# Another start for the top-k search, and one pass for its last places

## The reference

```python
s = jnp.einsum('bthd,bsd->bths', qi, ki)
score = jnp.einsum('bth,bths->bts', wi, jax.nn.relu(s))
visible = jnp.arange(L)[None, :] < limit[:, None]       # limit: the end of the row's chunk of 64
score = jnp.where(visible[None], score, -jnp.inf)
top_val, top_idx = lax.top_k(score, top_k)              # 256 of up to 2048; 144 of 576 for the sample
...
logits = jnp.einsum('btjgd,btnjd->btjgn', qg, k_sel) * (HEAD_DIM ** -0.5)
p = jax.nn.softmax(logits, axis=-1)
```

## Time and profile before

| | |
|---|---|
| median of three runs | 3711.19 us |
| span of the profiled execution | 3702.1 us |
| TensorE busy | 3263.2 us, 88% |
| VectorE busy | 2260.1 us, 61% |
| ScalarE busy | 1078.5 us, 29% |
| GpSimd busy | 785.9 us, 21% |
| mean granted TensorE clock | 0.952 |

### The profile page before, as it was taken

One profiled execution on the slowest core, in us unless ns is written; L12 is line 12 of the kernel. 1 busy time (PEld: TensorE's weight loads), 2 busy tenths in 40 slices (PEclk: granted clock), 3 DMA queues, 4 the chain that ended last, 5 costly groups with the idle time before them and its releaser, 6 DMA issues. The chain is left out here.

```text
span 3702.1 us, 51508 instructions
## 1 busy us (share of the span) xinstructions
PE 3263.2 (88%) x19482; PEld 2934.2 (79%) x19482; DVE 2260.1 (61%) x4788; ACT 1078.5 (29%) x1854; POOL 785.9 (21%) x404
## 2 busy tenths in 40 slices
PE   3999985787888887888789999999979899999997
PEld 2777764566666665667689999999969899999997
DVE  5667672777777766684226656656531666666654
ACT  2222222455455544444212221221221211211221
POOL 0000002111000000000245433433214434434420
PEclk7999996999999998999889999999989899999999
DMA  4122225221111010000321111111132211111101
GB/s 138 63 93 84 76 86 151 55 55 33 49 28 28 28 28 25 14 15 13 114 86 35 57 45 34 57 45 34 33 113 75 69 35 45 57 34 45 57 11 48
DMA packets 164909, 202.67 MB, mean 55 GB/s; under 512 B 27775, under 2 KB 138660, under 8 KB 162596
## 3 DMA queue, kind: packets, MB, share of 16 engines
q1 hardware_dynamic: 164772, 200.90, 17.2%
HBM read 155.61 MB, written 45.25 MB: 54 GB/s over the span
## 5 line engine op out<-in xcount | busy, mean ns | idle before, releaser
L1642 DVE SCALAR_TENSOR_TENSOR ffn_gv<-ffn_up,ffn_taps,ffn_gv 128x1056 f32<-128x1056 f32 (+2 forms) x264 | 418.5, 1599 | 157.0 <-ACT ffn_gv L1595 150.6
L1663 DVE TENSOR_TENSOR feed_hT<-feed_hT,ffn_ps_d 128x352 f32<-128x352 f32 x528 | 275.3, 522 | 329.1 <-PE ffn_ps_d L1548 329.1
L1535 PE MATMUL ffn_ps_u<-feed_nhi,feed_up_hi 128*128 128x352 f32 x2112 | 459.7, 326 | 15.8 <-DVE feed_nlo L1673 11.0
L1535 PE MATMUL ffn_ps_u<-feed_nhi,feed_up_lo 128*128 128x352 f32 x2112 | 456.6, 324 | 0.0
L1535 PE MATMUL ffn_ps_u<-feed_nlo,feed_up_hi 128*128 128x352 f32 x2112 | 456.2, 324 | 0.0
L1535 PEld LDWEIGHTS ffn_ps_u<-feed_nhi,feed_up_hi 128*128 128x128 f32 x2112 | 360.9, 190 | 19.3 <-DVE feed_nlo L1673 12.4
L1548 PE MATMUL ffn_ps_d<-ffn_a_hi,ffn_down_hi 128*128 128x352 f32 x1056 | 343.9, 326 | 29.3 <-DVE ffn_a_lo L1654 24.0
L1535 PEld LDWEIGHTS ffn_ps_u<-feed_nhi,feed_up_lo 128*128 128x128 f32 x2112 | 363.8, 188 | 0.0
L1535 PEld LDWEIGHTS ffn_ps_u<-feed_nlo,feed_up_hi 128*128 128x128 f32 x2112 | 360.2, 188 | 0.0
L862 POOL TENSOR_SCALAR att_diag<-ident,keep_w 128x128 f32<-128x128 f32 (+1 forms) x136 | 79.6, 606 | 1310.7 <-PE att_ps_s L892 800.6
L1548 PE MATMUL ffn_ps_d<-ffn_a_lo,ffn_down_hi 128*128 128x352 f32 x1056 | 343.0, 325 | 0.0
(11 more groups left out here) (258 smaller groups left out, 5964.5 us busy)
## 6 DMA issues: line engine op xcount, KB each, us to landing
feed_raw_up<-in_w_up SPq DMA_DIRECT2D x44, 1024.0 KB, 4.9
scratch_sT<-proj_sT SPq DMA_DIRECT2D x16, 1472.0 KB, 5.2
ffn_raw_down<-in_w_down SPq DMA_DIRECT2D x22, 1024.0 KB, 4.9
feed_nlo<-scratch_mixT SPq DMA_DIRECT2D x16, 528.0 KB, 7.7
proj_x<-in_x_prompt SPq DMA_DIRECT2D x16, 512.0 KB, 4.7
att_qi<-scratch_sT SPq DMA_DIRECT2D x16, 512.0 KB, 3.6
att_qa<-scratch_sT SPq DMA_DIRECT2D x16, 512.0 KB, 5.2
att_qb<-scratch_sT SPq DMA_DIRECT2D x32, 256.0 KB, 5.8
```

The lines of the kernel that those rows point to most:

```text
L1535: ins = pe.matmul(ps_u[:, half, s, 0:SUB], a[:, q, k, :], b[:, k, SUB * s:SUB * s + SUB], start=(k == 0 and n == 0), stop=(k == KC - 1 and ...
L1642: ins = dve.scalar_tensor_tensor(gv[:, half, lo:hi], up[:, lo + shift + j - 2:hi + shift + j - 2], taps[:, 2 * j + half, e:e + 1], gv[:, h ...
L1663: dve.tensor_tensor(at, at, ps_d[:, j % 2, 0:SUB], ALU.add).then_inc(partial_read[j % 2], 1)
```

## The change

Only `pick` and its helpers and tables change. The search begins not between minimum and maximum but at the mean plus z deviations, z being the normal quantile of the wanted share (table `guess`, one z and nine step widths for each row and block; the first step stands for 128 ranks, each later one for half). Mean and variance come from BN_STATS over pieces of 512 seen scores and BN_AGGR; the deviation from a reciprocal root with one refinement. There are 8 counts (`TRIES`), not 11. After the bound is found, the 8 largest scores below it are taken as before, and those that are still wanted are replaced in one MATCH_REPLACE; what is left above -0.5e30 becomes masked (`finish_mask`). The ranking of ties with `falling` (1024 KB once broadcast) is gone. A row that needs more than 8 places makes the branch `more_places` run, which does up to 16; beyond that `take_largest` as before. `pick` now has 13 parts, so in slots 6 and 7 of each block fewer stand.

```diff
-HALVINGS = 11
+TRIES = 8
+FIRST_STEP = 128.0
...
-            sp.dma_start(halves[:, :], t["halves"]).then_inc(tables_loaded, 16)
+            sp.dma_start(guess[:, :], t["guess"]).then_inc(tables_loaded, 16)
             sp.dma_start(places[:, :], t["places"]).then_inc(tables_loaded, 16)
-            sp.dma_start(falling[:, :], t["falling"].broadcast_to([P, SEQ])).then_inc(tables_loaded, 16)
...
                 if part == 0:
+                    for c, lo in enumerate(cuts):
+                        ins = dve.bn_stats(parts_of[0:T, c, :], scores[0:T, b.n % 2, lo:min(lo + 512, whole)])
                     dve.memset(failed[:, :], 0.0)
                     dve.memset(col(counts), 0.0)
-                    dve.tensor_reduce(col(low), row, AX.X, ALU.min)
-                    st.step(dve.tensor_reduce(col(mids), row, AX.X, ALU.max))
+                    dve.memset(col(mids), FAR)
...
+                    st.step(ins)
+                    st.step(dve.bn_aggr(about[0:T, :], parts_of[0:T, 0:len(cuts), :].rearrange("p c n -> p (c n)")))
...
-                elif part == HALVINGS + 2:
+                elif part == TRIES + 2:
                     st.step(dve.tensor_tensor(low_work, low_work, row, ALU.add))
-                    st.step(dve.max(top[0:T, :], low_work))
-                    st.step(dve.tensor_scalar(col(place), col(above), -1.0, b.keep - 1.0, ALU.mult, ALU.add))
...
+                    dve.tensor_scalar(failed[0:T, 0:1], col(place), 7.5, None, ALU.is_gt)
+                    dve.tensor_scalar(chosen[0:T, :], places[0:T, :], col(place), -FAR, ALU.is_gt, ALU.mult)
+                    st.step(dve.max(top[0:T, 0:8], low_work))
+                elif part == TRIES + 3:
+                    st.step(dve.tensor_tensor(chosen[0:T, 0:8], chosen[0:T, 0:8], top[0:T, 0:8], ALU.add))
+                    st.step(dve.match_replace(at, chosen[0:T, 0:8], low_work, -FAR))
+                    finish_mask(b, st)
+                elif part == TRIES + 4:
                     with dve.If(failed_rows(st) > 0):
-                        more_ties(b)
+                        more_places(b)
...
-                    st.step(dve.scalar_tensor_tensor(low_work, row, col(kth), falling[0:T, 0:S], ALU.is_equal, ALU.mult))
-                    st.step(dve.max(lowest[0:T, 0:8], low_work))
...
+            def finish_mask(b, own):
+                at = mask[0:b.T, b.n % 2, 0:b.S]
+                own.step(dve.tensor_scalar(at, at, -0.5 * FAR, MASKED, ALU.is_gt, ALU.mult))
+                if not b.sample:
+                    own.step(dve.memset(mask[0:CHUNK, b.n % 2, b.S - CHUNK:b.S], MASKED))
...
+            def more_places(b):
+                own.step(dve.match_replace(at, chosen[0:T, 0:8], low_work, -FAR))
+                own.step(dve.max(top[0:T, 8:16], at))
+                own.step(dve.tensor_tensor(chosen[0:T, 8:16], chosen[0:T, 8:16], top[0:T, 8:16], ALU.add))
+                own.step(dve.match_replace(low_work, chosen[0:T, 8:16], at, -FAR))
+                own.step(dve.tensor_copy(at, low_work))
+                finish_mask(b, own)
+                own.step(dve.tensor_scalar(failed[0:T, 0:1], place[0:T, 0:1], 15.5, None, ALU.is_gt))
```

More of the change, by code:

```diff
@@ L706, in phase_attend @@
         pT = m.sb("pT", [P, 2, NB, P])
[L707 to L715, removed]
+        top, idle = m.sb("top", [P, 16]), m.sb("idle", [P, 1])
+        mids, counts, steps = m.sb("mids", [P, TRIES + 1]), m.sb("counts", [P, TRIES + 1]), m.sb("steps", [P, TRIES + 1])
+        guess, places = m.sb("guess", [P, (NB + 1) * (TRIES + 2)]), m.sb("places", [P, 16])
+        parts_of, about = m.sb("parts_of", [P, 4, 6]), m.sb("about", [P, 2])
+        spread, square, back = m.sb("spread", [P, 1]), m.sb("square", [P, 1]), m.sb("back", [P, 1])
+        far, chosen = m.sb("far", [P, TRIES + 1]), m.sb("chosen", [P, 16])
+        bound, above, place = m.sb("bound", [P, 1]), m.sb("above", [P, 1]), m.sb("place", [P, 1])
         failed, failedT, failures = m.sb("failed", [P, 32]), m.sb("failedT", [P, 32]), m.sb("failures", [P, 1], I32)
@@ L1072, in pick @@
+                    st.step(dve.tensor_tensor(col(spread), col(spread), var, ALU.mult))
+                    dve.tensor_scalar(steps[0:T, :], z[:, 1:TRIES + 2], col(spread), None, ALU.mult)
+                    st.step(dve.scalar_tensor_tensor(col(mids, 1), z[:, 0:1], col(spread), col(about), ALU.mult, ALU.add))
+                elif part <= TRIES:
                     r = part
                     st.step(dve.tensor_scalar(low_work, row, col(mids, r), None, ALU.is_gt, ALU.add, accum_out=col(counts, r)))
-                    if r < HALVINGS:
+                    if r < TRIES:
@@ L1145, in take_largest @@
                 own = Steps(dve, general_steps)
-                own.step(dve.max(top[0:T, :], row))
-                own.step(dve.match_replace(cur, top[0:T, :], row, TAKEN))
+                own.step(dve.max(top[0:T, 0:8], row))
+                own.step(dve.match_replace(cur, top[0:T, 0:8], row, TAKEN))
                 rounds = b.keep // 8 - 1
@@ L1150, in take_largest @@
                     own.done = 2 + 2 * i
[L1151 removed]
+                    own.step(dve.max(top[0:T, 0:8], cur))
                     dve.memset(idle[:, :], 0.0)
[L1153 removed]
+                    own.step(dve.match_replace(cur, top[0:T, 0:8], cur, TAKEN))
                 own.done = 2 + 2 * rounds
@@ L1796, in program, with quantile @@
         store_conv(nc, t, ident, hist)
+def quantile(tail):
+    lo, hi = -8.0, 8.0
+    for _ in range(60):
+        z = 0.5 * (lo + hi)
+        lo, hi = (z, hi) if 0.5 * math.erfc(z / math.sqrt(2.0)) > tail else (lo, z)
+    return 0.5 * (lo + hi)
 def constants():
@@ L1816, in constants @@
         old.append(((s - P) > r - w)[96:] / f(w))
-    halves = np.broadcast_to(f(0.5) ** np.arange(1, HALVINGS + 1, dtype=f), (P, HALVINGS))
+    guess = np.zeros((P, NB + 1, TRIES + 2), f)
+    for b in BLOCKS:
+        for p in range(b.T):
+            seen = b.S if b.sample or p >= CHUNK else b.S - CHUNK
+            if b.keep:
+                z = quantile((b.keep - 4.5) / seen)
+                guess[p, b.n, 0] = z
+                guess[p, b.n, 1:] = FIRST_STEP / (seen * math.exp(-0.5 * z * z) / math.sqrt(2.0 * math.pi)) * 0.5 ** np.arange(TRIES + 1)
     places = np.broadcast_to(np.arange(16, dtype=f), (P, 16))
-    return {"halves": halves.astype(f), "places": places.astype(f), "falling": np.arange(SEQ, 0, -1, dtype=f)[None], "rope_table": np.concatenate(table, 1).astype(f), "band": np.array(band, f), "band_first": np.array(first, f),
+    return {"guess": guess.reshape(P, -1), "places": places.astype(f), "rope_table": np.concatenate(table, 1).astype(f), "band": np.array(band, f), "band_first": np.array(first, f),
             "band_old": np.array(old, f)}
```

43 lines of the change are left out of this document (13 added, 30 removed).

## The result

The changed kernel took 3667.0 us (median of 4, 3662.2 to 3670.9) against 3711.6 (3708.8 to 3716.4) for the kernel before on the same chip: a ratio of 0.9875, with a 95% interval of 0.9861 to 0.9889, or 44.6 us less. The same kernel, loaded and measured a second time (experiment after_again), took 3675.6 against 3714.6: ratio 0.9899 (0.9882 to 0.9915), 39.0 us less. The forecast was 3690, that is 21.6 us less: the direction is right and the gain is about double. The profiled execution of the first set has a span of 3668.7 us.

A forecast was written before the change was run, and what follows sets the result against it. The prediction took VectorE to bound block changes and TensorE the middle of late blocks. Terms of -3, -42.6, -13.7, +7, +14, +3 and +13.7 summed to -21.6 us, giving 3690 us, range 3676 to 3703.

The forecast's parts named there:

- 42.6 + 13.7: Block changes: 42.6 us of ordinary TensorE waits go, and 13.7 us of slow-clock loss behind them.
- The branch of block 2: Branch for rows lacking more than 8 places, at 384 keys: priced at 7.8 us.
- Rival A: VectorE's overruns in slot 5 and small blocks are absorbed by slack, giving 3666 us; chance 0.17.
- The tail of the pick moves two steps forward: Slots 6 and 7: the mask lies ready a head step early, removing 42.6 us of ordinary block-change waits.
- Blocks 2 and 6: +17.8: The branch was to run newly for one row each in these blocks, adding 17.8 us.
- two of them may drop the clock: Slot 5 in seven late blocks: two of its overruns may slow TensorE's clock, +3 us.
- slot 5's +14: From block 9 on, slot 5's work overruns TensorE's step by 2 us in seven blocks: +14 us (0 to 21).
- Rival B: The wait is moved to slot 5, not removed, and each such wait drops the clock: 3709 us, no change; chance 0.13.
- so 11 for 16.3: Block 13's branch: an 11 us wait replaces the old 16.3 us one.
- five in one for L1191: Of sixteen block changes before, five end in TensorE waiting for ps_o to be read, together 22.2 us.
- +7: Slots 4 to 6 in blocks up to 8: VectorE has no slack, so its net extra work adds 7 us.
- The start: Block 0: dropping the `falling` table's load shortens the first waits, -3 us (0 to -3.5).

The follow-up runs named there:

- late: The changed kernel with the pick's tail back at the end of the block (MATCH_REPLACE, mask and test in slot 7), eight counts kept: 3647.2 us.
- extra2w: The changed kernel with 11 tries and two dead passes over the row ahead of MATCH_REPLACE in slot 7: 3686.3 us, against 3639.3 without the passes.
- refine2: The changed kernel with one more Newton step for the deviation, so refined twice: 3677.5 us.
- no_test: The changed kernel without the test for missed rows and the branch behind it, tail still early: 3623.0 us.
- late_no_test: The changed kernel without the test for missed rows and its branch, with the tail at the end of the block: 3605.3 us.

## Why the prediction was right or wrong

*Right.* VectorE at the block changes was the bound, and TensorE's waits for it with the slow clock behind them were the prize. Forecast for both 42.6 + 13.7 = 56.3 us; from before to late, in the twelve of blocks 2 to 15 without a branch before (all but block 6, which runs block 7's pick, and block 12, which runs block 13's), 883.1 - 823.5 = 59.6. That these are so near is partly luck: the small blocks among them gave 14.6 and not the 9.9 of their waits. Slot 5 overruns in late blocks (forecast 14 and 3 of clock; 12.9 in the pair without test). BN_STATS is near one pass (1.97 us at 1536, 1.8 forecast). The branch of block 2: 7.8 forecast, 7.5 in the first profile (46.1 - 38.6), 4.6 in the second. Rival A, which has the nearest time (3666), is not what happened: the overruns are there.

*Wrong in its reason.* "The tail of the pick moves two steps forward ... the mask lies ready a head step early. The 42.6 us of ordinary waits go." This step failed. They go because the tail in slot 7 has two passes and four small instructions fewer (late; extra2w, where two passes bring 47.0 us back). The move itself costs: 1020.1 - 997.8 = 22 us in blocks 2 to 15. I had put the whole gain on the place, and so never asked what the shorter tail would do in the old one.

*Wrong in size*, in blocks 2 to 15, where -28.6 was forecast (the sum without the start's -3 and without some 10 for block 2's branch and overrun, which fall in block 1, and their clock) and -44.9 measured (-48.2 between the second executions):
- "Blocks 2 and 6: +17.8". Block 6 never ran it: 10 us and 1 of clock. My count took the exact deviation; the kernel refines its seed once, which moves the probes. By the count on the scores the worst row of block 6 then lacks one place less and stays within the eight; refine2, with one more refinement, runs the branch at 896 elements and pays 8.3 us in block 5. This is the largest error in the direction of the miss. The prices themselves were added up 0.4 too high: 3W + 2F + 4.9 is 7.4 at 384 and 9.6 at 896, not 7.8 and 10.0.
- "two of them may drop the clock", and slot 5's +14: in place the waits are 1.60, 1.65, 1.44, 1.43, none, none, 2.77, together 8.9; behind one of them the clock fell (at 1601.8 us). In lengths slot 5 costs 12.9 (no_test against late_no_test), 4 us less than the 17. Rival B held that each wait would drop the clock. Here four of 1.4 to 1.7 us had no slow stretch behind them, and the one of 2.77 had. The Trainium skill has idle gaps that return in each iteration pay the slow clock each time ("TensorE: Matmul & The Clock Gate", HAM oscillation), of a kernel whose gaps are longer than these; slot 5's waits don't bear it out.
- "so 11 for 16.3": block 13's branch leaves a wait of 7.17 (in block 12), 4 us less.
- "five in one for L1191": there are six. I missed 3.28 us at 1735.01, at the start of block 16; with it block 15 is 3.5 us shorter.
- "+7" in small blocks: too low. I took the difference of VectorE's instructions per slot, and named what waits behind head 8's maxima for the branch alone. The test stands there in every block, and ScalarE and TensorE wait for what is behind it: early against late costs 18.5 us in blocks 2 to 6. This is the largest error of all, and it hid part of the others.

With these, -28.6 - 11 - 4 - 4 - 3.5 + 13.5 (18.5 for the 5 that the +7 gave these blocks) is -37.6, and 7.3 us of the 44.9 are not placed. In the small blocks late gains more at the changes than the waits I had added up (14.6 against 9.9), which is a likely part of it, argued and not measured, and the kernel before is itself known to 3 us only in these blocks. *The start*: -3 forecast; block 0 took 25.3 and 24.6 us before and 24.1 and 24.6 after, and the table alone makes no difference, so no run shows this term. Block 16 took 30.3 to 43.5 us in the profiled executions, shorter where its clock was higher, which may be why the two sets of the changed kernel differ; it isn't shown, since only one execution of each was profiled. What decides its clock stays open.

## What to carry to other kernels

When a change both shortens a tail and moves it, price the two apart: here the shorter tail was worth 72 us by the median, and the move cost 22 in blocks 2 to 15. Before a test or branch is put early on an engine, look at which small result behind it another engine waits for; in blocks 2 to 6 a test of 4 us was free behind head 8's maxima and cost 4 us per block ahead of them. And read lengths block by block from two executions before believing a total: blocks 2 to 15 of the changed kernel repeated to 0.1 us where its medians lay 8.6 us apart, while the kernel before repeated in blocks 7 to 15 and was 3.2 us off in 2 to 6.

## What the hardware showed that I had not expected

- The same kernel in two sets of runs: block 16 at a granted clock of 1.00 in 30.3 us and at 0.56 in 43.5 us, with the same instructions; other variants had 34 or 42. Medians of the sets 3667.0 and 3675.6, with their runs within 9 and 3 us.
- The length of a wait of TensorE alone did not tell whether the clock fell behind it: in the changed kernel waits of 1.77, 2.02 and 1.91 us (ended at 1012.64, 1543.69 and 1632.26) had a stretch at 0.50 behind them, waits of 1.81, 1.81 and 1.84 (at 1086.84, 1335.60 and 1442.48) one at 1.00.
- Reading four values from SBUF into registers and branching holds VectorE for 3.4 to 3.8 us (the idle time before L1100, where the branch wasn't taken) whatever the row's width, as long as two passes over 1536 elements (3.5).
- The second dead pass in slot 7 cost 24.2 us in blocks 2 to 15, more than its 20.6 us of VectorE: TensorE's waits for masked logits rose from 28.3 to 42.8 us, and the time at half clock in blocks 7 to 15 from 37.8 to 49.6.
